# Merge stage begun inside the GLA scan, merged blocks, and zero images spread over the projection stage

## The reference, cut to what matters

```python
m = silu(c) @ w_mod + b_mod                      # 6 vectors: shift, scale, gate, shift2, scale2, gate2
h = modulate(rms_norm(x), m[0], m[1])            # the context with its own row of c
q, k, v, z, a, b, gq, gk, gv, gate, lr = split(h @ w_in)
o_a = gated_delta_net(silu(conv3(q, k, v)), a, b)    # 4 heads of 128, forward and backward, context first
o_b = gla(gq, gk, gv, lr)                            # 4 heads, dk 64, dv 128, forward and backward
y = concat(rms_norm(o_a) * silu(z), rms_norm(o_b) * silu(gate)) @ w_out
x = x + m[2] * y
h2 = modulate(rms_norm(x), m[3], m[4])
u = conv3x3(h2 @ w_up) ; x = x + m[5] * ((silu(u_a) * u_v) @ w_down)     # 2816 hidden channels
out = rms_norm(x)
```

## Time and profile before

| what | value |
|---|---|
| median of 3 runs | 1764.65 us (1762.67 to 1766.07) |
| the profiled execution | 1761.43 us |
| its span, first to last instruction | 1759.5 us |
| mean granted TensorE clock | 0.965 of full speed |
| busy: PE, PEld, DVE, ACT, POOL | 1645.4, 1224.1, 1223.1, 555.5, 441.9 us |

### The profile page before, as it was taken

One profiled execution on the slowest core, in us unless ns is written; L12 is line 12 of the kernel. 1 busy time (PEld: TensorE's weight loads), 2 busy tenths in 40 slices (PEclk: granted clock), 3 DMA queues, 4 the chain that ended last, 5 costly groups with the idle time before them and its releaser, 6 DMA issues.

```text
span 1759.5 us, 20882 instructions
## 1 busy us (share of the span) xinstructions
PE 1645.4 (94%) x8249; PEld 1224.1 (70%) x8249; DVE 1223.1 (70%) x1755; ACT 555.5 (32%) x890; POOL 441.9 (25%) x428
## 2 busy tenths in 40 slices
PE   7997999899989969999669989999999999999997
PEld 2544455886579946566457768888888888787886
DVE  2549777589545658888575549988988989633535
ACT  1533233445033322222334432222222222322332
POOL 4000000221023336656233343333333332200000
PEclk9998999989989979999879999999999999999999
DMA  9373554856198640000212321111111111532242
GB/s 336 91 278 106 170 180 143 247 133 156 24 273 247 202 143 13 25 24 13 107 45 89 108 61 48 48 48 50 51 51 52 49 48 37 204 99 96 96 141 84
DMA packets 202172, 194.23 MB, mean 110 GB/s; under 512 B 41045, under 2 KB 156063, under 8 KB 201948
## 3 DMA queue, kind: packets, MB, share of 16 engines
q1 hardware_dynamic: 194972, 187.40, 33.9%
q10 hardware_dynamic: 6816, 5.24, 1.0%
q0 software_dynamic: 288, 0.27, 0.0%
HBM read 150.77 MB, written 42.11 MB: 110 GB/s over the span
## 4 chain that ended last, share of the span: by engine, by line
PE 47%; DVE 7%; ACT 3%; DMA 2%; issue 2%; POOL 1%; SPq 0%; ACTq 0%; POOLq 0%
PE PS L2130 9%; PE PS L2128 9%; PE PS L2132 9%; PE PS L2165 4%; PE PS L2167 4%; PE PS L2169 4%; PE PS L1635 4%; PE PS L1648 2%; DVE Qbd L1846 2%; DMA ogb<-og_spill 2%; POOL xr L2325 1%; DVE AT L1862 1%; PE PS L1683 1%; DVE Ex L1827 1%; DVE oss L2357 0%
## 5 line engine op out<-in xcount | busy, mean ns | idle before, releaser
L2445 DVE SCALAR_TENSOR_TENSOR acc<-PS,fcol,acc 128x945 f32<-128x945 f32 (+2 forms) x176 | 215.2, 1222 | 35.2 <-ACT acc L2208 29.6
L2445 DVE SCALAR_TENSOR_TENSOR act<-PS,fcol,act 128x945 f32<-128x945 f32 (+2 forms) x176 | 215.1, 1222 | 21.6 <-ACT act L2208 16.2
L2128 PE MATMUL PS<-h2hi,whi 128*128 128x512 f32 x704 | 219.8, 390 | 0.0
L2130 PE MATMUL PS<-h2lo,whi 128*128 128x512 f32 x704 | 219.8, 390 | 0.0
L2132 PE MATMUL PS<-h2hi,wlo 128*128 128x512 f32 x704 | 219.6, 390 | 0.0
L389 PE MATMUL PS<-hT,wq 128*128 128x512 f32 (+1 forms) x432 | 163.3, 537 | 0.0
L2315 POOL TENSOR_TENSOR wlo<-wu,whi 128x1024 fp32r<-128x1024 f32 x44 | 106.4, 2420 | 216.5 <-ACT whi L2201 216.2
L2128 PEld LDWEIGHTS PS<-h2hi,whi 128*128 128x128 f32 x704 | 132.5, 188 | 27.4
L2132 PEld LDWEIGHTS PS<-h2hi,wlo 128*128 128x128 f32 x704 | 132.3, 188 | 27.5
L2130 PEld LDWEIGHTS PS<-h2lo,whi 128*128 128x128 f32 x704 | 132.3, 188 | 27.5
L2456 DVE TENSOR_TENSOR wrlo<-wr,wrhi 128x1024 fp32r<-128x1024 f32 x41 | 50.2, 1225 | 130.0 <-ACT wrhi L2271 129.9
(11 more groups left out here) (284 smaller groups left out, 2893.7 us busy)
## 6 DMA issues: line engine op xcount, KB each, us to landing
wm<-in_w_mod_dram SPq DMA_DIRECT2D x24, 1024.0 KB, 7.9
wu<-in_w_up_dram SPq DMA_DIRECT2D x44, 512.0 KB, 3.8
wr<-in_w_down_dram SPq DMA_DIRECT2D x44, 512.0 KB, 3.5
wq<-in_w_in_dram SPq DMA_DIRECT2D x12, 512.0 KB, 7.6
gdn_x_image<-ztile SPq DMA_DIRECT2D x10, 516.0 KB, 6.7
gdn_xt_image<-ztile SPq DMA_DIRECT2D x10, 516.0 KB, 6.5
GR<-gdn_gc_rows SPq DMA_DIRECT2D x20, 256.0 KB, 5.3
gdn_w_image<-Wm SPq DMA_DIRECT2D x20, 256.0 KB, 5.0
```

The costliest lines, as they stand in the source:

```text
L2128: pe.matmul(PS[:, b + half, :], whi[k][u][:, kk, :], h2hi[:, 4 * half:4 * half + 4, kk, :], start=(kk == 0), stop=False)
L2130: pe.matmul(PS[:, b + half, :], whi[k][u][:, kk, :], h2lo[:, 4 * half:4 * half + 4, kk, :], start=False, stop=False)
L2445: tp = v.scalar_tensor_tensor(out=t_[:, r0:r1, c0:c1], in0=up[:, r0 + dr:r1 + dr, c0 + dc:c1 + dc], scalar=tap_col(j, k, f), in1=t_[:, r0: ...
```

## The change

It has these parts:

- **Zero images**: in block 1 the six pieces per head are no longer issued ahead of the h spill and the w_mod blocks, but one or two after each block.
- **Blocks 2 and 3 become one**, and blocks 4 and 5 become one. The tiles of scan step 0 have places of their own (XT0, X0, W0), so SP fetches them when the solutions are stored, and the products of step 0's preparation stand between the units of K1. SP's fetch for step 1 waits for the last unit. TensorE waits for modulation_added ahead of K1.
- **decays_of(7)** moves behind ScalarE's copies of V1.1 and D0.
- **h** comes back into two tiles hL0 and hL1 (15 to 31 and 31 to 47 KB), fetched at once. The rows of w_out go to the same places: the first four when the last gate product on hL0 is done, the other four after that on hL1. og rows are fetched early in the GLA scan.
- **The gate row** is made at the start of the GLA scan (tile gdiag, banks 0 and 1, ahead of the first state products).
- **The last latent step** has no state products, no key decays and no state update, and its gate products all stand between the levels (`GATE_LAST`). `first(0)` stands in it, ahead of the last masked copy, and reads osq0.
- **Merge**: the token tiles are taken in the order 3, 4, 2, 1, 0, 5, 6, 7. Silu runs in two halves (`silus`), the first in `squares(0)`, the second after `squares(1)`; a gated product waits for its half. The low parts of w_out are all VectorE's.

```diff
                 for h in range(1, H):
                     load(h)
-                    zeros(6 * h - 4, 6 * h + 2)
                     if h == 1:
...
                     for i in range(4 * h - 1, min(4 * h + 3, 16)):
                         rest(i)
+                        zeros(2 + (i - 3) * 3 // 2, 2 + (i - 2) * 3 // 2)
...
+        XT0 = [place(f"XT0{d}", [P, HW], 178 + 2 * d) for d in range(2)]
+        X0 = [place(f"X0{d}", [P, HW], 182 + 2 * d) for d in range(2)]
+        W0 = [place(f"W0{d}", [P, HW], 186 + 2 * d) for d in range(2)]
...
+                for b in range(3):
+                    sp.wait_ge(s_xw[b], 64)
+                prep_in(0)
                 for u in range(2):
                     sp.wait_ge(s_as[u], 16 * NL)
+                sp.wait_ge(s_vs, 16)
+                sp.wait_ge(s_zs, 8)
+                sp.wait_ge(s_um, UNIT[("K", 0, 2)] + 1)
+                scan_in(0)
+                sp.wait_ge(s_um, len(UNITS))
+                sp.wait_ge(s_mq, 1)
+                prep_in(1)
+                scan_in(1)
...
-                tile("K1")
+                pe.wait_ge(s_m2d, 1)
+                unit(UNIT[("K", 1, 0)])
+                each(y32, 0)
+                unit(UNIT[("K", 1, 1)])
+                each(p32, 0)
+                unit(UNIT[("K", 1, 2)])
+                each(y64, 0)
+                pe.wait_ge(s_ue, len(UNITS))
+                each(turn, 0)
+                each(p64, 0)
...
-                decays_of(7)
                 evac(UNIT[("V", 1, 1)])
                 tile("D0")
+                decays_of(7)
                 tile("D1")
...
-                sp.dma_start(hT[:, :, 0:512], hT_dram[:, :, 0:512]).then_inc(s_hr, 16)
-                sp.wait_ge(s_hr, 16)
-                sp.dma_start(hT[:, :, 512:LAT], hT_dram[:, :, 512:LAT]).then_inc(s_hr, 16)
+                for half in range(2):
+                    sp.dma_start(hL[half][:, :, :], hT_dram[:, :, half * 512:(half + 1) * 512]).then_inc(s_hr[half], 16)
                 for n in range(1, 2 * H):
                     gate_weights(n)
-                sp.wait_ge(s_m4, 4 * H)
+                    if n == 1:
+                        for p in range(2):
+                            t = TORD[p]
+                            sp.dma_start(ogb[p][:, :], og_dram[t * P:(t + 1) * P, :]).then_inc(s_ogb[p], 16)
                 for k in range(KT):
-                    sp.dma_start(wo[:, k, :], w_out[0][k * P:(k + 1) * P, :]).then_inc(s_wo, 16)
+                    if k % 4 == 0:
+                        sp.wait_ge(s_m4, 4 * H - 1 + k // 4)
+                    sp.dma_start(wo[:, k, :], w_out[0][k * P:(k + 1) * P, :]).then_inc(s_wo[k], 16)
...
+                GATE_LAST = (None, (0, 0, 3), (0, 3, 6), (0, 6, 8), (1, 0, 3), (1, 3, 6), (1, 6, 8))
...
+                    if t == 0:
+                        pe.wait_ge(s_dg, 1)
+                        for k in range(KT):
+                            mm = pe.matmul(PS[:, k // 4, (k % 4) * P:(k % 4 + 1) * P], ones[:, :], gdiag[:, k * P:(k + 1) * P], start=True, stop=True)
+                        mm.then_inc(s_gbm, 1)
...
+                def silus(half):
+                    a.wait_ge(s_c4, 4 * H - 1 + half)
+                    for t in range(4 * half, 4 * half + 4):
+                        a.activation(sz[:, t, :, :], sz[:, t, :, :], ACT.Silu).then_inc(s_sz[half], 1)
...
                 squares(0)
-                a.wait_ge(s_wo, 16 * KT)
+                gate_copy(2 * H - 1, 1)
+                a.wait_ge(s_o2[0], NL)
                 for k in range(4):
                     w_high(k)
                 y_high(0)
                 for k in range(4, KT):
                     w_high(k)
                 squares(1)
+                silus(1)
...
-                for k in range(1, KT, 2):
+                for k in range(KT):
                     v.wait_ge(s_woh, k + 1)
                     v.tensor_tensor(wolo[:, k, :], wo[:, k, :], wohi[:, k, :], ALU.subtract).then_inc(s_wolv, 1)
...
-                pe.wait_ge(s_hlp, 4)
+                pe.wait_ge(s_hlp, 5)
```

More of the change, by code:

```diff
@@ new lines, in program @@
+        Vn = [place(f"Vn{d}", [P, HW], 166.25 + 2 * d) for d in range(2)]
+        Ys = [place(f"Ys{d}", [P, P], 170.25 + 2 * d) for d in range(2)]
+        Y2 = [place(f"Y2{d}", [P, 256], 192 + 2 * d) for d in range(2)]
+        og = place("og", [P, NL, HW], 176)
+        og_dram = nc.dram_tensor("og_spill", (LAT, HW), F32, kind="Internal").ap()
+        l_x, l_w, l_e, l_v, l_a = four("x_in"), four("w_in"), four("e_rows_in"), four("v_in"), four("a_in")
+        l_xt = [two(f"xt_in{i}") for i in range(3)]
@@ L928, in _, with bank, hd, y32 @@
                 mm.then_inc(s_mq, 1)
-                tile("K1")
+                def bank(d, n):
+                    return PS[:, 4 * d + n, :]
+                def hd(d, n, h):
+                    return PS[:, 4 * d + n, h * P:(h + 1) * P]
+                def y32(t, d):
+                    u = t % 2
+                    pe.wait_ge(l_x[u][d], 16 * (t // 2) + 16)
+                    pe.wait_ge(l_w[u][d], 16 * (t // 2) + 16)
+                    if t:
+                        pe.wait_ge(s_x2[d], t)
+                    for h in range(H):
+                        for q in range(2):
+                            b0, b1 = blocks(q, d)
+                            mm = pe.matmul(PS[b1, 4 * d + 3, h * BLK:(h + 1) * BLK], w_of(t, d)[b0, at_h(h, b1)], x_of(t, d)[b0, at_h(h, b0)],
+                                           start=True, stop=True)
+                    mm.then_inc(s_y[d], 1)
@@ new lines, in turn, with ks @@
+                def turn(t, d):
+                    c, at_ = chunk_of(d, t)
+                    if t:
+                        pe.wait_ge(s_vc[d], t)
+                    for h in range(H):
+                        tr = pe.transpose(hd(d, 2, h), kT[:, h, at_:at_ + P], ident[:, :])
+                    tr.then_inc(s_kt[d], 1)
+                def ks(t, d):
+                    c, at_ = chunk_of(d, t)
+                    pe.wait_ge(s_s[d], t + 1)
+                    for h in range(H):
+                        mm = pe.matmul(hd(d, 0, h), kT[:, h, at_:at_ + P], hs(S[d], h), start=True, stop=True)
+                    mm.then_inc(s_ks[d], 1)
@@ new lines, in each @@
+                def each(op, t):
+                    for d in range(2):
+                        op(t, d)
+                pe.wait_ge(s_m2d, 1)
[8 more added lines that the diff above has]
+                each(p64, 0)
+                for t in range(NT):
+                    lat, more = t >= NC, t + 1 < NT
+                    each(ks, t)
+                    if lat:
+                        each(qs, t)
+                    if more:
+                        each(y32, t + 1)
+                    each(vnew, t)
+                    if more:
+                        each(p32, t + 1)
+                    each(update, t)
+                    if more:
+                        each(y64, t + 1)
+                    if lat:
+                        each(av, t)
+                    if more:
+                        each(turn, t + 1)
+                        each(p64, t + 1)
```

1130 lines of the change are left out of this document (524 added, 606 removed).

## The result

The changed kernel takes 1726.06 us in the median of 4 runs (1722.54 to 1727.73) against 1764.54 for the kernel before, timed beside it (also 4 runs): a ratio of 0.978, with a 95% interval of 0.9761 to 0.9798. The prediction was 1727.5. The profiled execution took 1726.9 (span 1725.2), 34.5 less than that of before.

A forecast was written before the change was run, and what follows sets the result against it. It took waits and serial chains at five places, not products, to bound the kernel. Terms -8.5 - 5.3 - 6.5 + 3.5 - 20.3 = -37.1 put the profiled 1761.43 at 1724.3; plus 3.2, median 1727.5 us, range 1713 to 1744.

The forecast's parts named there:

- Zero images, -8.5: Block 1: spill and w_mod block ahead of the zeros shorten VectorE's and TensorE's waits; -8.5 us, ends -3.8 and -11.8.
- decays_of(7), -5.3: Block 2: ScalarE's copies go ahead of the late decays, so unit V1.2 starts earlier; -5.3 us, ends -2.6 and -7.7.
- Blocks 2 and 3, -6.5: GDN preparation and scan in one block: early tile fetch brings the first vnew forward; -6.5 us, ends -3 and -8.
- Gate row, +3.5: GLA scan start: scalings and products moved there delay the first state product; +3.5 us, ends 0 and +6.
- the dear end by the lock rule: GLA scan start: scalings take 5.86 us beside GpSimd on the shared port; +6 us, or +5 as term by that rule.
- Merge start, -20.3: GLA end to residual 0: hidden norm, early w_out, low parts on VectorE alone; -20.3 us, ends -12 and -24.
- the term without it: Merge start: no drain behind ScalarE's table loads, giving -20.3 us; with one exposed switch it would be -18.9.
- Rival D: GDN scan: TensorE falls to 1.2 GHz, losing about 10 us per step; eight steps give 1805 us; chance 0.03.

The follow-up runs named there:

- a1: Changed kernel with the six zero images per head put back ahead of the h spill and w_mod blocks: 1731.13 us, ratio 0.9813.
- a2: Changed kernel with decays_of(7) back ahead of ScalarE's copy of V1.1: 1732.83 us, ratio 0.9822.
- b2: Changed kernel with the 32 one-column products of the modulation placed two at a time between the k-steps of K0.0 and K0.1: 1725.51 us, ratio 0.9778.
- a4: Changed kernel with step 0's joining products (y32, p32, y64) behind all three units of K1, not between them: 1724.07 us, ratio 0.9775.
- b1: Changed kernel with the gate's 16 row products moved behind the first chunk's state products: 1719.62 us, ratio 0.9744.
- c1: Changed kernel with four edits together, those of b1, b2, a4 and b4: 1711.7 us, ratio 0.9699.
- c2: Changed kernel with all eight rows of w_out fetched only after the last gate product: 1722.33 us, ratio 0.9762.
- c3: Changed kernel with the first token tile's squares, first Silu half, sums and root behind the last attention product: 1732.17 us, ratio 0.9816.
- a3: Changed kernel with the even low rows of w_out on GpSimd again, the odd ones on VectorE: 1727.55 us, ratio 0.9793.
- b3: Changed kernel with token tiles in the order 3, 2, 4, 1, 0, 5, 6, 7 and Silu's second half behind y_high(1): 1728.43 us, ratio 0.9794.
- b4: Changed kernel with the fourth w_mod block issued ahead of the h spill: 1722.1 us, ratio 0.9753.

## Why the prediction was right, and where it was off

The sum was right in direction, in place and, within 3 us, in size. On the scale of the profiled executions it was -37.1 against -34.5; on that of the medians -37.2 against -38.5. The agreement of the medians is closer than the working deserves, and that is luck: I added 3.2 us because the profiled execution of before lies under its median, while that of after lies 0.8 above its own. The misses of the places also cancel in part: 1.7, 0.1, 1.1 and 2.3 us less gained than forecast, 1.1 and 1.4 more. Each place is measured in one pair of executions, and the start of the sums alone differs by 3.5 us between kernels that are equal up to it, so an agreement finer than 2 to 3 us at one place is not shown.

1. **Zero images, -8.5: measured -6.84.** The queue was read rightly: the block landed at 124.55 where 3.17 MB less put it at 123.5; VectorE waited 13.47 (predicted 12.6), TensorE 3.07 (2.2), and the sums took 3.04 (I took 0.8 off 3.78). a1 gives 6 to 7 back.
2. **decays_of(7), -5.3: measured -5.2** at V1.2. The wait moved to D1's copy behind the decays, as worked out. a2, which undoes this part alone, gives 3.6 of it back; its gap is 7.19 us where that of before was 8.61, so what else is in the 5.2 stays open. 1.1 were lost again in the units that follow, at a lower clock.
3. **Blocks 2 and 3, -6.5: measured -4.2.** This is the term that was mis-sized. From K1 on it was nearly right (-6.64, where the term has -7.1 behind its 0.6 for the bias), and the wait for modulation_added is there (0.28 us); but ahead of K1 2.4 us were lost, because the one-column products ran mostly at half the clock and took 10.55 instead of 8.54, and the wait takes its 0.3. The reordering was costed, the clock that it meets was not. Two errors cancel in the part from K1 on: y32 was to stand 1.4 us for W and stood for nothing, since K1.0 took about 10 us where the sum had 9 and the fetch went out at 458.08, as K1.0 began, where the sum had it 3 us later; and without the time lost to the clock the wait is there (b2). The reason for the gain was half wrong as well: step 0's products between the units do hide 1.9 us of the joining chain, but a4 shows that step 1's later fetch costs this and a little more before the first update.
4. **Gate row, +3.5: measured +2.4.** At the place the first state product stands 3.1 us later behind the turns. The scalings took 2.99, not 5.86, though GpSimd made Kde (1.54 us) while they ran: so the dear end by the lock rule of the Trainium skill (SBUF — State Buffer, "Who interferes with whom") did not come. The products took 3.78 on the path, as read from before. b1 shows that they needn't be there.
5. **Merge start, -20.3: measured -21.7.** Eight low parts took 9.16 (predicted 9.8), the second sums came 15.1 after the end of the attention product (16.1), residual 0 28.7 after it (29.9), and gated product 1 waited for the Silu half as worked out. But which part of the edit earns the 21.7 was not told apart. The runs do that in part. From the attention product to residual 0 the kernel gains 23.7 us, and 1.9 are lost ahead of it, where the gate products now stand. Undone one at a time, the hidden norm and Silu of the first tile give 9.2, the low parts on VectorE alone 0.6, w_out in halves 0.1. The other 12 must lie in the rest: the gate row gone from the merge, the og rows that are there in time, the last gate products gone from behind the attention product (3.6 us before), and the second Silu half, which the first tile no longer waits for. These were not tried one by one, and pieces undone singly need not add up. The Trainium skill (ScalarE: Activation LUTs, "What ACT_TABLE_LOAD costs") has a drain of about 1.38 us behind a load; here the Silu starts at 870.57, 0.01 after the load that began at 869.28 ended. The trace doesn't show a drain, and the term without it was the nearer one.

Rival D, the lower clock in the GDN scan, was not idle: in step 0 it costs about 3 us in some traces; in none does it go through eight steps.

## What to carry to other kernels

Cost a reordering of a queue or of an engine's list place by place, at the instruction that waits, and add the shifts: four of five terms came within 1.7 us here. Then test each piece of a bundle by undoing it: here three pieces (w_out in halves, the low parts on one engine, products between units) gave next to nothing on balance. When an undone piece moves nothing, look whether two effects cancel before calling it idle, and compare stretches at the same granted clock. Look for what shares a wait before adding two gains: spreading the one-column products paid nothing until the products behind them were moved off the landing of W.

## What was unexpected on the chip

**One-column products draw the clock down.** 64 records of a 128 by 1 product in a row (32 products, two records each) start at a granted clock of 1.00 and end at 0.50 (1.2 GHz) in every trace that has them so, and the 512-column products behind them stay there for another 3 to 6 us (6.2 in the changed kernel). Placed by two products between the k-steps of 512-column products (c1, b2) four records take 0.50 us, against 0.66 in the run, and the clock stays at 1.00 up to K1's end (c1's windows above).

**Scan step 0 runs at either clock.** In the nine traces whose code from K1 to the first update is that of the changed kernel, the distance is 31.3 to 32.0 us where vnew and the first update take 2.05 each (a1, b1, c2, c3), 34.6 to 34.9 where both take about 3.78 (a2, a3, b3), and between them where vnew alone is long (the changed kernel 34.04, of which about 1 us is K1.0's longer stay at the lower clock; b4 33.29). The windows of a2 and a1 from 490 to 500 us, with the granted clock third from the end:

```profile
490.00:500.00 10.00, 7.57 (x105) 6.97 (x104) 3.68 (x15) 3.32 (x8) 2.08 (x2) 0.64 1.06 302
```

```profile
490.00:500.00 10.00, 7.69 (x139) 7.05 (x139) 5.97 (x24) 3.85 (x10) 2.04 (x2) 1.00 1.11 313
```

TensorE is busy as long in both, the clock is not the same. The 3 us are as much as an interval of a ratio is wide to one side, and probably a good part of the 5 us and more by which executions of one kernel differ; only one execution of each was traced, so that share is not shown. Medians alone could not rank a3, a4, b2, b3 and c2. What tips it stays open.
